# Transposes ahead of both down products, and a rearranged last expert and final norm

## The chip, the cores and the metric

The kernel runs on one core of one Trainium2 chip. The metric is the device time of one execution in microseconds. The core has a matrix engine (TensorE, "PE" in the profile), a vector engine (VectorE, "DVE"), a scalar engine (ScalarE, "ACT"), GpSimd ("POOL"), and SyncE ("SP"), whose queue issues nearly all DMAs here. Matrix products take a stationary operand of up to 128 rows (the contracted dimension) by 128 columns and a moving operand of up to 512 columns, and write into one of 8 banks of the accumulator memory (PSUM), which is `ps[:, bank, :]` in the code. A tile of 64 columns or 64 rows uses half of the array.

## The reference, cut to what matters

One encoder layer on 256 tokens of width 1024, in float32: norm, one wide projection, attention and a recurrent branch, merge, output projection, residual. Then the part that fills most of the time, a mixture of 32 experts, 4 of them for each token, and a last norm:

```python
h = rmsnorm(x, norm2_g);  logits = h @ w_router + b_router
top_val, top_idx = top_k(logits, 4);  gates = softmax(top_val)
for each expert e, on the tokens routed to it:
    gu  = xb @ w_gu[e] + b_gu[e]              # 1024 -> 2048
    g, u = split(gu);  g = minimum(g, 7);  u = clip(u, -7, 7)
    act = g * sigmoid(1.702 * g) * (u + 1)
    y  += gate * (act @ w_down[e] + b_down[e])   # 1024 -> 1024, added at the token's row
x = x + y
return rmsnorm(x, final_g)
```

Every expert's weights are 12 MiB (8 for `w_gu`, 4 for `w_down`), so 384 MiB of weights are read from the chip's memory once.

## The kernel before, in words

The mixer in front of the experts takes the first 240 us or so. All weights come in chunks of 2 MiB, 128 partitions by 16 KiB. Expert e has six: four of `w_gu`, two of `w_down`. They land in a ring of eight slots (`SLOT_ORDER`; the eighth is called `wide`), and SP issues the load of a chunk when the chunk that had its slot before has been used: it waits on `chunk_used[j]`, which TensorE raises after the products of a chunk (`expert_load` L293, `loop_load` L341). Two chunks of step 3 (`EXTRA`, numbers 18 and 19) have places of their own beside the ring. So in step 3 two gate/up products free no slot.

There is one step for each expert, `step(n, i)` on each engine; `i` counts modulo 4, and one set of 4 steps is a turn of a loop after the first 4. In step n TensorE does, in this order: gate/up product 0 of expert n (`gate_up`, L1333, 8 products of 128x64 tiles, two of them side by side), the gather of the tokens of expert n+1 by a 0/1 matrix (`gather_tile`, L1286), gate/up 1, in odd steps the transposes of the gate matrix (L1365) and two scatter products (L1305), gate/up 2, the transposes of the gathered tokens (`gathered_transposes`, L1300), in odd steps two more scatter products, gate/up 3, down product 0 of expert n-1 (`down`, L1342), the transposes of expert n's gate/up result (L1387), and down product 1 of expert n-1. The down products of an expert so run one step later than its gate/up. In step 0 (`first`), which has no down product, two products put the residual into banks 2 and 3 (`residual_in_bank`, L1264).

The transposes of L1387 wait until VectorE (L987) and ScalarE (L558) have each copied half of the gate/up result out of PSUM. VectorE then adds the bias and clamps (L993 to L998), ScalarE takes the sigmoid (L560), VectorE multiplies (L1001, L1005), and `act_ok` lets the next step's down products go. The next step's first gate/up product waits until L993 has read the transposes (`tp_read`).

Two experts share a `pair_out` tile, one in rows 0 to 63, one in rows 64 to 127, so that one scatter product of 128 rows adds two experts into banks 0 to 3, which hold the residual stream. For the last pair this happens at the end: TensorE does the down products of expert 31 (the second chunk in four quarters, L352), ScalarE and VectorE copy its result (L551, L1017), four scatter products follow (L1305), and then the final norm: ScalarE squares a tile of 128x1024 with a sum (L577), VectorE adds epsilon and inverts (L594, L595), ScalarE takes the root (L371), VectorE multiplies by root and gain (L1024), and SP stores 256 KB at a time (L357).

Order on each engine is that of its program. SP's queue is in order too.

Of the kernel before, what the change touches and what calls it, by code (L numbers as in the profile page):

```python
# [19 lines left out]
P = 128  # L20
# [35 lines left out]
def encoder_layer(nc, x, consts, squares, rows, pre, w_lru, w_gu, w_down, b_down, out):  # L56
# [5 lines left out]
    with ctx:  # L62
# [104 lines left out]
        bdn, gateT = pair_out[1][0:NE, :], sgT[1][0:NE, :, :]  # L167

# [42 lines left out]
        fin_ok, zeros = sem("fin_ok"), sem("zeros_ok")  # L211
        mix_part = sem("mix_part")
        last_in = [sem(f"last_quarter_in{r}") for r in range(4)]
        last_out = sem("last_out_v")
# [55 lines left out]
        LAST_SLOT = SLOT_ORDER[-3 % SLOTS]  # L270
        LAST_AFTER = (lambda nj: (nj[0] + (1 if nj[1] < 4 else AHEAD), nj[1]))(divmod(1 - SLOTS, PER))
# [7 lines left out]
        def _(sp):  # L279
# [69 lines left out]
            loop_load(n_pass, 0, 0, 4, NE - 1)  # L349
            sp.wait_ge(chunk_used[LAST_AFTER[1]], sp.snap(n_pass + LAST_AFTER[0]))  # L350
            for r in range(4):
                sp.dma_start(slot(LAST_SLOT)[:, r * D:(r + 1) * D],  # L352
                             expert_src(NE - 1, 5)[:, r * D:(r + 1) * D]).then_inc(last_in[r], 16)
# [8 lines left out]
        def _(act):  # L362
# [183 lines left out]
            def down_copy(n, i, bank=6, sides=range(2)):  # L546

                at_least(dn_done, n + 1 + AHEAD)
                rs = slice(64 * (i % 2), 64 * (i % 2) + 64)
                for side in sides:  # L550
                    nc.scalar.activation(pair_out[i // 2 % 2][rs, side * BANK:(side + 1) * BANK],  # L551
                                         ps[64 * side:64 * side + 64, bank, :], ACT.Copy).then_inc(out_ok, 1)
# [20 lines left out]
            down_copy(n_pass - 1, UNROLL - 1, 4, [0])  # L573

            for t in range(T):
                act.wait_ge(y_ok, 2 * t + 2)
                nc.scalar.activation(lruA[:, t * D:(t + 1) * D].rearrange("p (b n) -> p b n", b=2),  # L577
                                     ps[:, 2 * t:2 * t + 2, :], ACT.Square,
                                     accum_out=ssum[:, t:t + 1]).then_inc(sq_sum, 1)
                root(4 + t, slice(t, t + 1))  # L580

        @block.vector
        def _(dve):
# [389 lines left out]
            def step(n, i):  # L973
# [11 lines left out]
                scale_gathered(n + 1, i + 1)  # L985
                dve.wait_ge(gu_done, n1)
                nc.vector.tensor_copy(gu_sb[:, 0:BANK], ps[:, 4, :]).then_inc(gu_v, 1)  # L987
                dve.wait_ge(tp_ps, n1)
# [26 lines left out]

            dve.wait_ge(dn_done, dve.snap(n_pass + AHEAD))
            nc.vector.tensor_copy(pair_out[1][64:128, BANK:2 * BANK], ps[64:128, 4, :]).then_inc(last_out, 1)  # L1017
            dve.wait_ge(late_in, 32)
            for t in range(T):
                inverse_variance(ssum[:, t:t + 1], 2 * T + t + 1)  # L1020
                dve.wait_ge(rstd_ok, 4 + t)
                for h in range(2):
                    cols = slice(h * BANK, (h + 1) * BANK)
                    nc.vector.scalar_tensor_tensor(out=x_sb[:, t, cols], in0=ps[:, 2 * t + h, :], scalar=rstd[:, t:t + 1],  # L1024
                                                   in1=fin_g[:, cols], op0=ALU.mult, op1=ALU.mult).then_inc(fin_ok, 1)
# [3 lines left out]
        def _(pe):  # L1029
# [323 lines left out]
            def step(n, i, first=False):  # L1353
# [16 lines left out]
                if first:  # L1370
                    residual_in_bank(2)
                    residual_in_bank(3)
                gathered_transposes(n + 1)
# [4 lines left out]
                if not first:  # L1378
                    at_least(act_ok, n)
                    if i % 2 == 1:  # L1380
                        at_least(sg_ok, n + 3)
                    at_least(out_ok, n * 2 + 1)
                    down(n, i, 0, 4)
# [5 lines left out]
                if not first:  # L1389
                    down(n, i, 1, 5)  # L1390
# [22 lines left out]
            down(n_pass, 0, 0, 0, 4)  # L1413
# [74 lines left out]
```

## Time and profile before

| | |
|---|---|
| time, median of 3 runs | 1166.57 us |
| the three runs | 1162.07, 1166.57, 1167.43 us |
| span of the profiled execution (first to last instruction) | 1161.2 us |
| TensorE busy | 93% |
| VectorE, ScalarE busy | 33%, 20% |
| read from the chip's memory | 438.46 MB, 378 GB/s over the span |
| mean granted TensorE clock | 0.994 |

The profiled execution gives its span, 1161.2 us, and no time of its own beside it; of the timed runs the lowest, 1162.07 us, is 0.9 us above this span, and the other two are 5.4 and 6.2 us above it. A row of a timeline has start, duration, engine, line, operation, output and inputs, number of instructions, and in brackets the idle time before and what ended it. A float32 product is two instructions. Durations of a group overlap the next one's start by about 0.15 us (the end of the last product is counted with its way through the array), so that the time a group takes in a busy stretch is read from start to start.

### The profile page before, as it was taken

What the parts mean: (1) busy time and instruction counts of PE and PEld (TensorE: products, weight loads), DVE (VectorE), ACT (ScalarE), POOL (GpSimd) and SP (SyncE); (2) the same over time, 40 slices, a digit from 0 to 9 for tenths busy, and PEclk for the clock granted to TensorE, in tenths of its full rate; (3) what the DMA queues carried; (4) which work ended last, traced back from release to release, by engine and by line L of the source; (5) the groups of instructions that cost most, each with busy time, mean ns of one, the idle gap of its engine ahead of it and who ended that gap; (6) DMA issues with size and microseconds to landing.
All of it is one profiled execution on the core that took longest, in us unless ns stands there. A gap on an engine that the chain in (4) does not pass through costs nothing.

```text
span 1161.2 us, 13145 instructions
## 1 busy us (share of the span) xinstructions
PE 1081.6 (93%) x5391; PEld 502.8 (43%) x5391; DVE 382.9 (33%) x671; ACT 234.2 (20%) x371; POOL 0.2 (0%) x4
## 2 busy tenths in 40 slices
PE   5998999989999999999998989898989898989997
PEld 5998789823333333333333323332333233323332
DVE  6996798532322222222121212121211212121122
ACT  5388843100111111111111111111110101010112
POOL 0000000000000000000000000000000000000000
PEclk9999999989999999999999999999999999999999
DMA  8543146998999999999999999999999999999996
GB/s 351 186 171 145 73 160 278 418 400 333 429 397 425 431 425 429 428 428 429 428 429 428 430 428 427 430 428 428 430 428 428 429 428 430 428 427 429 429 428 248
DMA packets 32618, 439.89 MB, mean 379 GB/s; under 512 B 3760, under 2 KB 3888, under 8 KB 5712
## 3 DMA queue, kind: packets, MB, share of 16 engines
q1 hardware_dynamic: 32112, 438.53, 89.9%
q10 hardware_dynamic: 480, 0.99, 0.2%
q8 instruction: 19, 0.31, 0.1%
q14 instruction: 7, 0.06, 0.0%
HBM read 438.46 MB, written 1.05 MB: 378 GB/s over the span
## 4 chain that ended last, share of the span: by engine, by line
PE 61%; DMA 33%; DVE 4%; ACT 1%; issue 1%; SPq 0%; DVEq 0%
DMA slot<-in_w_gu_dram 27%; PE ps L1333 25%; PE ps L1037 12%; PE ps L1342 10%; DMA slot<-in_w_down_dram 6%; PE ps L1305 4%; PE ps L1286 3%; PE ps L1300 1%; PE ps L1387 1%; DVE slot_r L627 1%; PE ps L1092 1%; PE ps L1135 1%; PE ps L1264 1%; PE ps L1156 1%; PE ps L1365 0%
## 5 line engine op out<-in xcount | busy, mean ns | idle before, releaser
L1333 PE MATMUL ps<-slot,lru 128*64 128x512 f32 x880 | 198.9, 595 | 21.0 <-DMA slot<-in_w_gu_dram 20.7
L1342 PE MATMUL ps<-slot,lru 128*64 128x512 f32 x896 | 203.3, 596 | 14.8 <-DMA slot<-in_w_down_dram 14.3
L1333 PE MATMUL ps<-slot,qT 128*64 128x512 f32 x880 | 202.1, 601 | 14.4 <-DMA slot<-in_w_gu_dram 12.9
L1333 PEld LDWEIGHTS ps<-slot,lru 128*64 128x64 f32 x880 | 62.7, 137 | 147.6 <-issue 113.5
L1333 PEld LDWEIGHTS ps<-slot,qT 128*64 128x64 f32 x880 | 62.5, 137 | 147.1 <-issue 134.9
L1342 PEld LDWEIGHTS ps<-slot,lru 128*64 128x64 f32 x896 | 62.3, 137 | 135.4 <-issue 117.1
L558 ACT ACTIVATE lru<-ps 128x512 f32<-128x512 f32 x32 | 19.1, 598 | 419.7 <-PE ps L1333 419.7
L993 DVE TENSOR_TENSOR lru<-ps,cst 128x1024 f32<-128x1024 f32 x32 | 39.2, 1225 | 141.5 <-PE ps L1387 141.5
L970 DVE TENSOR_SCALAR lru<-sq,x_sb,small 128x64 f32<-128x64 f32 x66 | 17.7, 312 | 188.1 <-PE ps L1286 188.1
L1037 PE MATMUL ps<-wide_r,slot_r 128*128 128x256 f32 x492 | 66.2, 286 | 0.2 <-DVE slot_r L627 0.2
L1305 PE MATMUL ps<-lru 128*128 128x512 f32 x136 | 63.9, 593 | 0.9 <-DVE lru L1017 0.9
L1286 PE MATMUL ps<-hn,lru 128*64 128x512 f32 x264 | 63.7, 600 | 0.9 <-DVE lru L907 0.9
L987 DVE COPY lru<-ps 128x512 f32<-128x512 f32 x32 | 22.1, 692 | 127.6 <-PE ps L1333 127.6
L1037 PEld LDWEIGHTS ps<-wide_r,slot_r 128*128 128x128 f32 x492 | 61.3, 191 | 4.6 <-issue 4.1
L560 ACT ACTIVATE lru<-lru 128x512 f32<-128x512 f32 x32 | 20.2, 632 | 198.3 <-DVE lru L997 198.3
L627 DVE TENSOR_TENSOR slot_r<-slot,slot_r 128x4096 fp32r<-128x4096 f32 (+1 forms) x14 | 59.7, 4268 | 0.3 <-ACT slot_r L386 0.2
L544 ACT ACTIVATE qT<-ps 128x512 f32<-128x512 f32 x33 | 19.7, 598 | 160.7 <-PE ps L1286 160.7
L937 DVE TENSOR_TENSOR qT<-ps,cst 128x512 f32<-128x512 f32 x16 | 11.1, 692 | 116.6 <-PE ps L1300 116.6
L386 ACT ACTIVATE slot_r<-slot 128x2048 fp32r<-128x2048 f32 (+1 forms) x24 | 43.1, 1838 | 22.1 <-DMA slot<-in_pre_dram 22.1
L551 ACT ACTIVATE lru<-ps 64x512 f32<-64x512 f32 x63 | 37.3, 592 | 39.4 <-PE ps L1342 38.7
L1387 PEld LDWEIGHTS ps<-sq,lru 128*128 128x128 f32 x256 | 30.9, 193 | 26.8 <-issue 25.2
L937 DVE TENSOR_TENSOR lru<-ps,cst 128x512 f32<-128x512 f32 x17 | 11.8, 692 | 89.5 <-PE ps L1300 89.5
(212 smaller groups left out, 905.1 us busy)
## 6 DMA issues: line engine op xcount, KB each, us to landing
slot<-in_w_gu_dram SPq DMA_DIRECT2D x110, 2048.0 KB, 34.9
slot<-in_w_down_dram SPq DMA_DIRECT2D x55, 2048.0 KB, 33.2
wide<-in_w_gu_dram SPq DMA_DIRECT2D x15, 2048.0 KB, 34.8
slot<-in_pre_dram SPq DMA_DIRECT2D x14, 2048.0 KB, 8.3
wide<-in_w_down_dram SPq DMA_DIRECT2D x8, 2048.0 KB, 35.3
slot<-in_w_lru_dram SPq DMA_DIRECT2D x2, 1024.0 KB, 13.3
wide<-in_w_gu_dram SPq DMA_DIRECT2D x2, 1024.0 KB, 14.8
late<-in_w_gu_dram SPq DMA_DIRECT2D x1, 2048.0 KB, 16.8
```

The costliest lines, as they stand in the source:

```text
L386: nc.scalar.activation(high(c)[:, i * w:(i + 1) * w], whole(c)[:, i * w:(i + 1) * w], ACT.Copy).then_inc(split_hi, 1)
L551: nc.scalar.activation(pair_out[i // 2 % 2][rs, side * BANK:(side + 1) * BANK], ps[64 * side:64 * side + 64, bank, :], ACT.Copy).then_inc( ...
L627: return nc.vector.tensor_tensor(dst, whole, hi.bitcast(f32), ALU.subtract)
L937: nc.vector.tensor_tensor(xgT[i % 2].rearrange("p (h k) n -> p k h n", h=2), ps[:, 7, :].rearrange("p (k h n) -> p k h n", k=KD // 2, h=2) ...
L987: nc.vector.tensor_copy(gu_sb[:, 0:BANK], ps[:, 4, :]).then_inc(gu_v, 1)
L993: nc.vector.tensor_tensor(gub.rearrange("p (j n) -> p j n", j=16), ps[:, 4:6, :].rearrange("p b (j n) -> p (b j) n", n=CAP), bias.unsqueez ...
L1037: ins = nc.tensor.matmul(dst, st[a], mv[b], start=start and q == 0 and k == 0, stop=stop and q == 2 and k == len(sides) - 1)
L1286: ins = nc.tensor.matmul(ps[64 * h:64 * h + 64, 7, :], sel_next[:, t, :], x2[:, t, h * BANK:(h + 1) * BANK], start=(t == 0), stop=(t == T ...
L1305: return nc.tensor.matmul(ps[:, n, :], sgT[pair][:, n // 2, :], pair_out[pair][:, (n % 2) * BANK:(n % 2 + 1) * BANK], start=False, stop=last)
L1333: ins = nc.tensor.matmul(ps[64 * side:64 * side + 64, 4 + b, :], xgT[i % 2][:, k, :], rows[r][:, o:o + BANK], start=(k == 0), stop=(k == K ...
L1342: ins = nc.tensor.matmul(ps[64 * side:64 * side + 64, bank, :], actT[(i - 1) % 2][:, k, :], w[:, r, side * BANK:(side + 1) * BANK], start= ...
L1387: ins = nc.tensor.transpose(ps[:, 4 + j // 4, j % 4 * P:(j % 4 + 1) * P], gu_sb[:, j::KD], ident)
```

## The change

In each expert step on TensorE the transposes of the gathered tokens move behind gate/up 3, the transposes of the gate/up result come directly after them, and both down products come behind these. On VectorE the copy of the gate/up half goes ahead of the scaling of the gathered tokens. In step 0 one residual product stands between the two sets of transposes and one behind them. At the end both chunks of the last `w_down` are loaded and multiplied in quarters; expert 30 is scattered alone, by four products of 64 rows, between quarters 2 and 3 of the last chunk; the gate matrix of expert 31 is made once more so that it stands in both halves of the rows; expert 31 is scattered as pairs of 64-row tiles, one in the upper rows for the left 512 columns and one in the lower rows for the right 512. The last norm squares 512 columns at a time and VectorE multiplies by the gain first (in place of one product by both factors) and by the root in a second turn.

```diff
         def landed(c):
             return slot_full[PLACE[c]], 16 * PLACE[:c + 1].count(PLACE[c])
-        LAST_SLOT = SLOT_ORDER[-3 % SLOTS]
-        LAST_AFTER = (lambda nj: (nj[0] + (1 if nj[1] < 4 else AHEAD), nj[1]))(divmod(1 - SLOTS, PER))
+        LAST_SLOTS = [SLOT_ORDER[(j - 2 - len(EXTRA)) % SLOTS] for j in range(2)]
+        LAST_AFTER = [(nj[0] + (1 if nj[1] < 4 else AHEAD), nj[1]) for nj in (divmod(j - SLOTS, PER) for j in range(2))]
         def expert_src(e, j):
             c = gu_chunk[e, j] if j < 4 else dn_chunk[e, j - 4]
...
                     e_before = sp.snap(sp.to_reg((n + i - 1) & (NE - 1)), min_val=0, max_val=NE - 1)
                     for j in range(PER):
                         loop_load(n, i, j, j, e if j < 4 else e_before)
-            loop_load(n_pass, 0, 0, 4, NE - 1)
-            sp.wait_ge(chunk_used[LAST_AFTER[1]], sp.snap(n_pass + LAST_AFTER[0]))
-            for r in range(4):
-                sp.dma_start(slot(LAST_SLOT)[:, r * D:(r + 1) * D],
-                             expert_src(NE - 1, 5)[:, r * D:(r + 1) * D]).then_inc(last_in[r], 16)
+            for j, (after, used) in enumerate(LAST_AFTER):
+                sp.wait_ge(chunk_used[used], sp.snap(n_pass + after))
+                for r in range(4):
+                    sp.dma_start(slot(LAST_SLOTS[j])[:, r * D:(r + 1) * D],
+                                 expert_src(NE - 1, 4 + j)[:, r * D:(r + 1) * D]).then_inc(last_in[4 * j + r], 16)
             for n in range(2 * T):
                 t, cols = n // 2, slice((n % 2) * BANK, (n % 2 + 1) * BANK)
                 sp.wait_ge(fin_ok, n + 1)
...
                 at_least(xg_ps, n + 1)
                 nc.scalar.activation(xg_sb, ps[:, 7, :], ACT.Copy).then_inc(xg_cp, 1)
-            def down_copy(n, i, bank=6, sides=range(2)):
+            def down_copy(n, i):
                 at_least(dn_done, n + 1 + AHEAD)
                 rs = slice(64 * (i % 2), 64 * (i % 2) + 64)
-                for side in sides:
+                for side in range(2):
                     nc.scalar.activation(pair_out[i // 2 % 2][rs, side * BANK:(side + 1) * BANK],
-                                         ps[64 * side:64 * side + 64, bank, :], ACT.Copy).then_inc(out_ok, 1)
+                                         ps[64 * side:64 * side + 64, 6, :], ACT.Copy).then_inc(out_ok, 1)
             def step(n, i, first=False):
...
                 for i in range(UNROLL):
                     step(n + i, i)
             load_sqrt_table(3)
-            down_copy(n_pass - 1, UNROLL - 1, 4, [0])
+            act.wait_ge(dn_done, act.snap(n_pass + AHEAD))
+            nc.scalar.activation(last_pair[0:64, :], ps[0:64, 4, :], ACT.Copy).then_inc(out_ok, 1)
             for t in range(T):
                 act.wait_ge(y_ok, 2 * t + 2)
-                nc.scalar.activation(lruA[:, t * D:(t + 1) * D].rearrange("p (b n) -> p b n", b=2),
-                                     ps[:, 2 * t:2 * t + 2, :], ACT.Square,
-                                     accum_out=ssum[:, t:t + 1]).then_inc(sq_sum, 1)
-                root(4 + t, slice(t, t + 1))
+                for h in range(2):
+                    if h == 1:
+                        act.wait_ge(fin_y, 2 * t + 1)
+                    nc.scalar.activation(lruA[:, t * D + h * BANK:t * D + (h + 1) * BANK], ps[:, 2 * t + h, :], ACT.Square,
+                                         accum_out=part_sum[:, 2 * t + h:2 * t + h + 1]).then_inc(sq_sum, 1)
+            for t in range(T):
+                act.wait_ge(var_inv, 4 + t)
+                nc.scalar.activation(rstd[:, t:t + 1], ssum[:, t:t + 1], ACT.Sqrt, scale=float(D)).then_inc(rstd_ok, 1)
         @block.vector
         def _(dve):
...
                     dve.wait_ge(sg_ps, n1)
                     nc.vector.tensor_copy(sgT[i // 2], ps[:, 6, 0:T * P].rearrange("p (t n) -> p t n", t=T)
                                           ).then_inc(sg_ok, 2)
-                scale_gathered(n + 1, i + 1)
                 dve.wait_ge(gu_done, n1)
                 nc.vector.tensor_copy(gu_sb[:, 0:BANK], ps[:, 4, :]).then_inc(gu_v, 1)
+                scale_gathered(n + 1, i + 1)
                 dve.wait_ge(tp_ps, n1)
                 if isinstance(n, int):
                     bias = cst[:, C_BGU + 16 * n:C_BGU + 16 * (n + 1)]
...
                     step(n + i, i)
+            for t in range(T):
+                nc.vector.tensor_scalar(sel_gate[:, t, 0:CAP], slotno[:, 0:CAP], rank_col[:, t, column(n_pass - 1)],
+                                        gate_col[:, t, column(n_pass - 1)], ALU.is_equal, ALU.mult).then_inc(sgate_ok, 1)
+            dve.wait_ge(sg_ps, dve.snap(n_pass + 1))
+            nc.vector.tensor_copy(last_sgT, ps[:, 7, 0:T * P].rearrange("p (t n) -> p t n", t=T)).then_inc(last_sg, 1)
             dve.wait_ge(dn_done, dve.snap(n_pass + AHEAD))
-            nc.vector.tensor_copy(pair_out[1][64:128, BANK:2 * BANK], ps[64:128, 4, :]).then_inc(last_out, 1)
+            nc.vector.tensor_copy(last_pair[64:128, :], ps[64:128, 4, :]).then_inc(last_out, 1)
             dve.wait_ge(late_in, 32)
-            for t in range(T):
-                inverse_variance(ssum[:, t:t + 1], 2 * T + t + 1)
+
+            def with_gain(t):
+                for h in (1, 0):
+                    cols = slice(h * BANK, (h + 1) * BANK)
+                    if h == 1:
+                        dve.wait_ge(y_ok, 2 * t + 2)
+                    else:
+                        dve.wait_ge(sq_sum, 2 * T + 2 * t + 1)
+                    nc.vector.tensor_tensor(x_sb[:, t, cols], ps[:, 2 * t + h, :], fin_g[:, cols],
+                                            ALU.mult).then_inc(fin_y, 1)
+
+            def last_variance(t):
+                dve.wait_ge(sq_sum, 2 * T + 2 * t + 2)
+                link(nc.vector.tensor_scalar(ssum[:, t:t + 1], part_sum[:, 2 * t:2 * t + 1], part_sum[:, 2 * t + 1:2 * t + 2],
+                                             D * EPS, ALU.add, ALU.add))
+                nc.vector.reciprocal(ssum[:, t:t + 1], ssum[:, t:t + 1]).then_inc(var_inv, 1)
+
+            def normalize(t):
                 dve.wait_ge(rstd_ok, 4 + t)
+                dve.wait_ge(fin_y, 2 * t + 2)
                 for h in range(2):
                     cols = slice(h * BANK, (h + 1) * BANK)
-                    nc.vector.scalar_tensor_tensor(out=x_sb[:, t, cols], in0=ps[:, 2 * t + h, :], scalar=rstd[:, t:t + 1],
-                                                   in1=fin_g[:, cols], op0=ALU.mult, op1=ALU.mult).then_inc(fin_ok, 1)
+                    nc.vector.tensor_scalar(x_sb[:, t, cols], x_sb[:, t, cols], rstd[:, t:t + 1], None,
+                                            ALU.mult).then_inc(fin_ok, 1)
+
+            with_gain(0)
+            last_variance(0)
+            with_gain(1)
+            last_variance(1)
+            normalize(0)
+            normalize(1)
         @block.tensor
...
                     scatter(1 - i // 2, 0)
                     scatter(1 - i // 2, 1)
                 gate_up(n, i, 2)
-                if first:
-                    residual_in_bank(2)
-                    residual_in_bank(3)
-                gathered_transposes(n + 1)
                 if i % 2 == 1:
                     scatter(1 - i // 2, 2)
                     scatter(1 - i // 2, 3)
                 gate_up(n, i, 3)
-                if not first:
-                    at_least(act_ok, n)
-                    if i % 2 == 1:
-                        at_least(sg_ok, n + 3)
-                    at_least(out_ok, n * 2 + 1)
-                    down(n, i, 0, 4)
+                gathered_transposes(n + 1)
+                if first:
+                    residual_in_bank(2)
                 at_least(gu_v, n + 1)
                 at_least(gu_a, n + 1)
                 for j in range(KD):
                     ins = nc.tensor.transpose(ps[:, 4 + j // 4, j % 4 * P:(j % 4 + 1) * P], gu_sb[:, j::KD], ident)
                 ins.then_inc(tp_ps, 1)
-                if not first:
-                    down(n, i, 1, 5)
+                if first:
+                    residual_in_bank(3)
+                    return
+                at_least(act_ok, n)
+                if i % 2 == 1:
+                    at_least(sg_ok, n + 3)
+                at_least(out_ok, n * 2 + 1)
+                down(n, i, 0, 4)
+                down(n, i, 1, 5)
             pe.wait_ge(sel_ok, 1)
             gather_tile(0)
...
                 for i in range(UNROLL):
                     step(n + i, i)
             pe.wait_ge(act_ok, pe.snap(n_pass))
-            down(n_pass, 0, 0, 0, 4)
-            for r in range(4):
-                pe.wait_ge(last_in[r], 16)
-                ins = down_rows(0, LAST_SLOT, 1, r, 4)
+            for j in range(2):
+                for r in range(4):
+                    pe.wait_ge(last_in[4 * j + r], 16)
+                    ins = down_rows(0, LAST_SLOTS[j], j, r, 4)
+                    if (j, r) == (0, 2):
+                        pe.wait_ge(sgate_ok, pe.snap(n_pass * T + T))
+                        pe.wait_ge(xg_ok, pe.snap(n_pass + 1))
+                        for t in range(T):
+                            dup = nc.tensor.transpose(ps[:, 7, t * P:(t + 1) * P], sel_gate[:, t, :], ident)
+                        dup.then_inc(sg_ps, 1)
+                    if (j, r) == (1, 1):
+                        pe.wait_ge(out_ok, pe.snap(n_pass * 2 + 1))
+                        for n in range(2 * T):
+                            nc.tensor.matmul(ps[:, n, :], sgT[1][0:CAP, n // 2, :],
+                                             pair_out[1][0:CAP, n % 2 * BANK:(n % 2 + 1) * BANK], start=False, stop=False)
             ins.then_inc(dn_done, 1)
             pe.wait_ge(out_ok, pe.snap(n_pass * 2 + 2))
             pe.wait_ge(last_out, 1)
-            for n in range(2 * T):
-                scatter(1, n, True).then_inc(y_ok, 1)
+            pe.wait_ge(last_sg, 1)
+            for t in range(T):
+                for h in range(2):
+                    rs = slice(64 * h, 64 * h + 64)
+                    nc.tensor.matmul(ps[:, 2 * t + h, :], last_sgT[rs, t, :], last_pair[rs, :],
+                                     start=False, stop=True).then_inc(y_ok, 1)
 # ---- launch: layouts only ----
```

## Rows read from the trace of the kernel before

**Rows 1.** The page, span in 40 equal slices: memory rate.
```profile
GB/s 351 186 171 145 73 160 278 418 400 333 429 397 425 431 425 429 428 428 429 428 429 428 430 428 427 430 428 428 430 428 428 429 428 430 428 427 429 429 428 248
```

**Rows 2.** Windows: stretch, length, busy time per engine, granted clock, DMA share, GB/s.
```profile
398.00:551.00 153.00, 153.00 (x706) 54.32 (x704) 33.50 (x66) 17.44 (x29) 0.00 (x0) 1.00 1.01 428
610.00:668.00 58.00, 52.76 (x239) 18.82 (x237) 11.90 (x23) 6.02 (x10) 0.00 (x0) 1.00 1.01 429
340.00:342.00 2.00, 2.00 (x12) 0.62 (x9) 0.00 (x0) 0.00 (x0) 0.00 (x0) 1.00 0.56 238
264.00:266.00 2.00, 2.00 (x7) 0.62 (x5) 1.63 (x3) 0.58 (x1) 0.00 (x0) 0.51 0.93 393
1147.00:1148.00 1.00, 1.00 (x8) 0.38 (x6) 0.00 (x0) 0.00 (x0) 0.00 (x0) 1.00 0.28 115
1157.00:1158.00 1.00, 0.00 (x0) 0.00 (x0) 0.73 (x3) 0.20 (x1) 0.00 (x0) 1.00 1.00 377
```

**Rows 3.** Waits of PE, 560 to 1095 us: total, times, longest.
```profile
PE ps L1333 <- DMA slot<-in_w_gu_dram: 32.2, 33, 1.3
```

**Rows 4.** Timeline of SP, 330 to 345 us: the one issue there.
```profile
341.79 0.33 SPq L293 DMA_DIRECT2D slot<-in_w_gu_dram  x1
```

**Rows 5.** Timeline of PE, steps 4 and 5, start of step 6.
```profile
346.26 3.60 PE L1333 MATMUL ps<-slot,lru 128*64 128x512 f32 x16
...
358.38 0.66 PE L1300 MATMUL ps<-sq,qT 128*128 128x128 f32 x4
358.96 3.65 PE L1333 MATMUL ps<-slot,lru 128*64 128x512 f32 x16
...
370.56 3.60 PE L1333 MATMUL ps<-slot,qT 128*64 128x512 f32 x16
...
398.81 0.60 PE L1333 MATMUL ps<-slot,lru 128*64 128x512 f32 x2
```

**Rows 6.** Timeline of PE, end of step 0 and start of step 1.
```profile
252.51 3.71 PE L1264 MATMUL ps<-hn,sq 128*128 128x512 f32 x4
...
256.59 3.65 PE L1333 MATMUL ps<-wide,lru 128*64 128x512 f32 x16
261.04 1.15 PE L1387 MATMUL ps<-sq,lru 128*128 128x128 f32 x8 [0.80 <-DVE lru L987]
263.70 5.35 PE L1333 MATMUL ps<-slot,qT 128*64 128x512 f32 x16 [1.52 <-DVE lru L993]
268.86 0.63 PE L1286 MATMUL ps<-hn,lru 128*64 128x512 f32 x2
```

**Rows 7.** Timeline of PE, step 31 to the last scatter.
```profile
1119.09 0.14 PEld L1333 LDWEIGHTS ps<-slot,qT 128*64 128x64 f32 x2 [0.32 <-DMA slot<-in_w_gu_dram]
...
1130.99 3.65 PE L1333 MATMUL ps<-slot,qT 128*64 128x512 f32 x16
...
1138.01 1.16 PE L1387 MATMUL ps<-sq,lru 128*128 128x128 f32 x8
1139.10 3.65 PE L1342 MATMUL ps<-wide,lru 128*64 128x512 f32 x16
...
1143.56 7.09 PE L1342 MATMUL ps<-slot,lru 128*64 128x512 f32 x32 [0.81 <-DMA slot<-in_w_down_dram]
...
1151.54 3.67 PE L1305 MATMUL ps<-lru 128*128 128x512 f32 x8 [0.89 <-DVE lru L1017]
```

**Rows 8.** Timeline of ACT, DVE and SP, the last norm.
```profile
1156.15 2.93 SPq L357 DMA_DIRECT2D out_dram<-x_sb  x4
1156.17 0.19 ACT L577 ACTIVATION_READ_ACCUMULATOR lru<-ps 128x1 f32 x1
...
1157.31 1.41 DVE L1024 SCALAR_TENSOR_TENSOR x_sb<-ps,small,lru 128x512 f32<-128x512 f32 x2 [0.27 <-ACT small L371]
```

**Rows 9.** The page, costliest groups: a copy and a scaling of 128x512.
```profile
L558 ACT ACTIVATE lru<-ps 128x512 f32<-128x512 f32 x32 | 19.1, 598 | 419.7 <-PE ps L1333 419.7
...
L997 DVE TENSOR_SCALAR lru<-lru 128x512 f32<-128x512 f32 x32 | 13.7, 427 | 1.1
```

More of the change, by code:

```diff
@@ L167, in encoder_layer @@
         bdn, gateT = pair_out[1][0:NE, :], sgT[1][0:NE, :, :]
+        part_sum = neg_max
+        last_pair, last_sgT = pair_out[0][:, 0:BANK], sgT[0]
         gv = gub.rearrange("p (j h n) -> p j h n", j=KD, h=2)
@@ L210, in encoder_layer @@
             sem(n) for n in ("g_clamped", "sigmoid_ok", "u_clamped", "gated_ok", "act_ok", "out_ok", "y_ok"))
-        fin_ok, zeros = sem("fin_ok"), sem("zeros_ok")
+        fin_y, fin_ok, zeros = sem("fin_y"), sem("fin_ok"), sem("zeros_ok")
         mix_part = sem("mix_part")
-        last_in = [sem(f"last_quarter_in{r}") for r in range(4)]
-        last_out = sem("last_out_v")
+        last_in = [sem(f"last_quarter_in{r}") for r in range(8)]
+        last_out, last_sg = sem("last_out_v"), sem("last_sgT_ok")
         block = ctx.enter_context(nc.Block())
```

## The prediction

> **What bounds the kernel now.** I read the memory rate over the span first [rows 1]. From the thirteenth slice to the last but one it stands at 425 to 431 GB/s; before that, between 232 and 348 us, it drops twice (333 and 397). Then two windows [rows 2]. From 398 to 551 us TensorE is busy all of the time and the DMA share is 1.01. From 610 to 668 us the DMA share is the same and TensorE has 5.2 of 58 us idle. So the weight stream runs without a gap in both, and TensorE, which is behind it at first, has caught up by 560 us and waits for chunks from then on [rows 3]. A pair of steps costs TensorE 52.55 us (346.26 to 398.81), of which the even one takes 24.30 and the odd one 28.25 [rows 5], a mean of 26.3. The stream needs 12 chunks of 2.097 MB at 428.5 GB/s, 58.7 us for a pair or 29.36 for a step. Between step 4 and the end, TensorE could be later by a good 1.8 us in each step without being the bound (from 346.26 to 1142.6 there are 28 steps, 28.4 us each, against 26.3, and the change adds 0.3, below).
>
> Three things therefore set the end: when the stream last ran dry, since from there it only flows; how long TensorE still works behind the last chunks; and the norm. The last dry place is at 340 to 343 us, where the DMA share of a window is 0.56 [rows 2] and SP issues a load at 341.79 after a long wait [rows 4]. It is the slot that down product 0 of step 3 sets free (two chunks of that step lie outside the ring and free nothing). At the other end TensorE waits for a gate/up chunk at 1119.09 and then works without a pause until a wait of 0.81 us ahead of 1143.56 [rows 7], while the stream is almost over by 1147 to 1148 [rows 2]. TensorE goes on to 1150.65. The last 7 us of products are TensorE's own.
>
> **Start, step 0.** Now gate/up 3 starts at 252.51, where the two residual products stand, instead of 256.59: 4.08 earlier [rows 6]. A gate/up group takes 3.5 from start to start (3.65 less the 0.15 of overlap), the transposes of the gathered tokens 0.58 (358.38 to 358.96 [rows 5]), a residual product 1.77 (half of the time from 252.51 to 256.59, less 0.58). Before, the transposes of the gate/up result followed 4.45 after the start of gate/up 3, with 0.80 idle for the copies; now gate/up, transposes and residual fill 5.85, so the wait is covered, and they start at 258.36. From these transposes to step 1's first product it was 2.66 (261.04 to 263.70), with 1.52 idle for VectorE's read; a residual product behind transposes of 1.09 (1138.01 to 1139.10 [rows 7]) fills 2.86. Step 1 begins at 261.2, 2.5 earlier.
>
> The group there took 5.35 in place of 3.65, and its window shows a granted clock of 0.51 (1.2 GHz) [rows 2, 6]. The engine had been idle for 0.80 and 1.52 just before, with only the transposes between. These idle times go, so I take the full clock: the next group starts 3.5 instead of 5.16 later, and the gain is 4.1. If the low clock stays it is 2.5.
>
> **Every further step.** The transposes of the result start 4.45 after gate/up 3 starts [rows 6], as the copies need that; 3.5 plus 0.58 of the moved transposes fill 4.08. So 0.37 is idle that the down product covered before. Two sets of the same tile shape now stand together, which spares a change of shape; I take 0.3 a step, with 0 and 0.5 as ends. VectorE's scaling of the gathered tokens comes later but is covered by both down products (7.0). The down products find their input from the step before, and the two copies of the down result are still made after the second. No DMA is added. What depends on the new place is the release of the slots: gate/up 3 frees its slot 0.58 earlier, down product 0 by 1.09 plus the wait later, down product 1 about 0.3 later.
>
> At the dry place: 4.1 gained, 3 steps of 0.3 lost (1, 2 and 3), 1.1 lost as the transposes stand ahead of down product 0. The issue at 341.79 comes 2.1 earlier, and the stream with everything that waits for it to 1119.09 moves by that. Ends: 0.5 (low clock) and 3.0 (no wait in the steps). The mean step of 26.3 becomes 26.6, still under 28.4, and costs nothing there.
>
> A page of the Trainium skill, "TensorE: Matmul & The Clock Gate" (Part 4, PE-mode transpose), says that transposes do not count as activity for the clock in the way that matmuls do. By that rule the change brings two sets together with a wait between them in every step, and the clock could fall there; the rival on the clock is priced below.
>
> **Tail, from step 31.** Rows 7 give it. Before: gate/up 3 at 1130.99, transposes at 1138.01, second down product at 1139.10, its successor possible at 1142.6, started at 1143.56 when the chunk had landed, 7.09, end 1150.65. After, on the same clock: gate/up 3 at 1130.41 (0.58 of transposes gone ahead of it), transposes 4.45 later at 1134.86, down products from 1135.95 to 1142.95. The quarters of the first last chunk are in by 1143.5 and three come before, so nothing waits for the 0.81 any more. Then TensorE has eight quarters, 6.95; two transposes of the gate matrix, a quarter of eight, 0.3, and 0.1 for the shape; and the four scatter products of expert 30. These have 64 rows, but 512 moving columns as before and all in the same half of rows, so I give them the time of the 128-row ones, 3.55 of 3.67 [rows 7]. Sum 142.95 + 6.95 + 0.4 + 3.55 + 0.15 of drain = 1154.0, or 3.35 later than 1150.65. Ends: 1.6, if 64 rows cost half, and 3.9, if each of the four changes of shape costs another 0.14. The eight quarters have 4 KB rows; SP may stand at the issue, but nothing is behind it there save the stores.
>
> The step was made to take those products out of the very end. There, four products side by side in two halves of rows cost half of 3.67, a gain of 1.8 for the last data. The same 3.55 now stands before, and no supply wait covers it.
>
> **Norm.** From the scatter's start S (1151.54, 0.89 after the down product) to VectorE's end it took 7.18 [rows 7, 8]. After: the first tile is complete at S+1.0, the second at 1.9. ScalarE's half square is 0.60 [rows 9] and 0.19 to read the sum [rows 8], 0.8 with the handover; VectorE's product from PSUM 0.70 (half of 1.41). The two alternate over the two halves: VectorE to 1.7, ScalarE to 2.65, VectorE's sums to 3.05, gain product to 3.75, the fourth square to 4.65, sums to 5.1; the second turns, 0.43 each with overlap [rows 9], end at 6.7. That is 0.45 less. But the first store goes at 5.6, where it went at 4.6 (1156.15), and four stores of 0.7 (262 KB at 377 GB/s [rows 2]) then stand in a row of 2.8: 0.45 more by the stores. I take nothing, with 0.5 either way. That 64-row tiles in different halves run together no row shows; in turn they take 3.67 and the second tile is 0.9 later than ScalarE comes to it. Column tiles do run in pairs: 16 instructions of L1333 take 3.65, where 8 of L1305 take 3.67.
>
> **Sum.** -2.1 (start) + 3.35 (tail) + 0 (norm) = +1.3 us, on the profiled span of 1161.2: 1162.5. The span is 5.4 below the median of the runs, and I move the median by the same: 1166.57 + 1.3 = 1168.
>
> **The rivals.**
> (a) The low clock at the start of step 1 stays, or comes elsewhere among the first steps: start 0.5 instead of 2.1. +2.9, 1169.5. For it: no row tells how little idle time suffices. Against: in the stream-paced steps idle times of 1.3 [rows 3] stand once in some groups and the mean clock is still 1.00 [rows 2]. 15%.
> (b) The row tiles don't run in pairs: +0.9 on the norm, +2.2, 1169. 8%.
> (c) The tail costs nothing: the scatter of expert 30 falls into time in which TensorE waits for quarters. Then -2.1, 1164.5. Against it, no wait in the 23 us after 1119.09 but one of 0.81. 10%.
> (d) Faster by over 0.5%: the stream loses 10.5 us against 428.5 GB/s in the four slices from 232 to 348 (28.5, 95.5 and 31.5 GB/s missing of slices of 29.03 us, [rows 1]). If an earlier gate/up 3 closed most of it and not one gap alone, 6 to 9 us, less the tail: 1160. Against: the last gap hangs on down product 0 of step 3, whatever comes before. 7%.
> (e) Slower: the clock falls within the steps. Place: the two sets of transposes with the wait, in steps 4 to 31; price 1.7 (5.35 less 3.65 [rows 6]) for each group that runs at 1.2 GHz. One a step gives 28.3, still under 28.4, and costs only 1.7 or so at the tail. It decides above 1.8 us a step; two groups make 30.0, 28 steps of 1.6, +45 us, 1212. For it, the row at 263.70. Against, the stretch without ordinary products is 0.58 + 0.37 + 1.09 = 2.0, and at 263.70 it was 3.5 (0.80 + 1.15 + 1.52). 5%.
> The rest, 55%, is the forecast.
>
> **How the numbers follow.** The forecast with its ends (start -3.0 to -0.5, tail 1.6 to 3.9, norm -0.5 to 0.5) runs from -1.9 to +3.9 and with (b) to +4.8; the three runs of before spread over 5.4 us, and a median of three may fall on either side of it. I give 1162 to 1173. Under 0.5% (5.8 us) the measurement of this kernel can't tell a change from none. Faster by more: (d) and a little of (c), 8%. Slower by more: (e), and a tenth of the rest by a bad sum of its upper ends, 11%. Same: 81%.
>
> **What would show it.** In the changed kernel's profile: step 1's first group at about 261.2 of 3.65 at clock 1.00, and none at 0.51 near 264; an idle time of 0.3 to 0.4 ahead of the transposes of each step, ended by VectorE's copy; the issue after the two extra chunks at 339.7, and the waits for chunks at the same phase as before but 2 us earlier; no wait for a quarter, the end of the down products 10.6 to 11.5 after the second down product of step 31 ends; a scatter of 8 instructions at the end in 1.9. I am wrong if the start gains under 0.5 or over 3, if TensorE waits for quarters, or if steps in the stream-paced stretch take other than 58.7 a pair.

## The result, and the profile after

The changed kernel takes 1167.13 us (median of 20 runs, 1163.53 to 1170.3), the kernel before 1164.44 us in the 20 runs beside it (1161.6 to 1167.43). The ratio is 1.003, with a 95% interval of 1.0021 to 1.0039: some 3.5 us (2.4 to 4.5) slower, and under the 0.5% that I had called no change. I had forecast +1.3 us and 1168. That 1168 lies close to 1167.13 is luck: the median of three runs that I started from (1166.57) is 2.1 us above the median of 20 (1164.44), and the change is 2.2 us larger than I had. One execution of 2252.93 us (the kernel before) and one of 2841.81 us (steps 1 to 31 alone) are far outside the others and are left out of every median, mean and ratio here. The two profiled executions are only 0.5 apart, 1161.2 and 1161.7, so at least one of them must differ from the usual run, and the question is where.

To compare them I cut the span at events that both have: SP's issue of the first `w_down` chunk (it waits for step 0's first product), SP's issue after the two extra chunks, the first gate/up product of step 31, the end of the last down product (the copy on VectorE starts 0.05 later), and the end of the span. SP's timeline of the kernel before, with the first of these; the second is [rows 4]:

```profile
244.04 5.48 SPq L293 DMA_DIRECT2D slot<-in_w_down_dram  x2
```

SP's timeline of the changed kernel:

```profile
243.22 5.48 SPq L295 DMA_DIRECT2D slot<-in_w_down_dram  x2
...
338.75 0.33 SPq L295 DMA_DIRECT2D slot<-in_w_gu_dram  x1
```

From one to the other it is 97.75 before and 95.53 after: 2.2 less. TensorE at the end of step 0, changed kernel, for [rows 6]:

```profile
251.60 3.60 PE L1369 MATMUL ps<-wide,lru 128*64 128x512 f32 x16
255.13 0.66 PE L1336 MATMUL ps<-sq,qT 128*128 128x128 f32 x4
255.62 1.89 PE L1300 MATMUL ps<-hn,sq 128*128 128x512 f32 x2
257.34 1.07 PE L1416 MATMUL ps<-sq,lru 128*128 128x128 f32 x8
258.24 1.89 PE L1300 MATMUL ps<-hn,sq 128*128 128x512 f32 x2
260.06 3.65 PE L1369 MATMUL ps<-slot,qT 128*64 128x512 f32 x16
263.54 1.89 PE L1322 MATMUL ps<-hn,lru 128*64 128x512 f32 x8
```

No row has a bracket, so both idle times of [rows 6] are covered. Step 1's first group takes 3.65 in place of 5.35. Then the tail. The first product of step 31 and VectorE's copy behind the last down product, in the kernel before, which [rows 7] does not show:

```profile
1114.28 3.65 PE L1333 MATMUL ps<-slot,qT 128*64 128x512 f32 x16 [1.33 <-DMA slot<-in_w_gu_dram]
...
1150.70 0.69 DVE L1017 COPY lru<-ps 64x512 f32<-64x512 f32 x1 [7.64 <-PE ps L1342]
```

The changed kernel, step 31 and the end:

```profile
1111.01 3.65 PE L1369 MATMUL ps<-slot,qT 128*64 128x512 f32 x16 [1.34 <-DMA slot<-in_w_gu_dram]
...
1130.91 0.66 PE L1336 MATMUL ps<-sq,qT 128*128 128x128 f32 x4
...
1131.78 1.17 PE L1416 MATMUL ps<-sq,lru 128*128 128x128 f32 x8 [0.21 <-DVE lru L993]
1132.87 3.65 PE L1378 MATMUL ps<-slot,lru 128*64 128x512 f32 x16
...
1136.36 3.60 PE L1378 MATMUL ps<-wide,lru 128*64 128x512 f32 x16
...
1139.79 2.75 PE L1378 MATMUL ps<-slot,lru 128*64 128x512 f32 x12
...
1142.46 0.44 PE L1457 MATMUL ps<-sq,lru 128*128 128x128 f32 x2
1142.83 2.80 PE L1378 MATMUL ps<-slot,lru 128*64 128x512 f32 x12
1145.56 3.70 PE L1462 MATMUL ps<-lru 64*128 64x512 f32 x8
1149.18 1.94 PE L1378 MATMUL ps<-slot,lru 128*64 128x512 f32 x8
...
1151.97 1.99 PE L1471 MATMUL ps<-lru 64*128 64x512 f32 x8 [0.84 <-ACT lru L576]
```

Expert 30's scatter stands at 1145.56 and takes 3.62 to the next start, although its stationary tile has 64 rows; expert 31's, in pairs, takes 1.99 for as many instructions. None of the rows with quarters (1139.79, 1142.83, 1149.18) has a bracket: TensorE waits for no quarter. From 1111.01 to the end of the down products (1151.12) it is 40.11; before, from 1114.28 to 1150.65, it was 36.37. That is 3.74 more.

The stream in those last microseconds (window of the changed kernel: stretch, length, busy times, clock, DMA share, GB/s) had ended by 1145:

```profile
1145.00:1150.00 5.00, 5.00 (x16) 1.76 (x14) 0.00 (x0) 0.00 (x0) 0.00 (x0) 1.00 0.00 0
```

The norm, for [rows 8]:

```profile
1151.17 0.69 DVE L1029 COPY lru<-ps 64x512 f32<-64x512 f32 x1 [7.81 <-PE ps L1378]
...
1156.74 1.67 DVE L1053 TENSOR_SCALAR x_sb<-x_sb,small 128x512 f32<-128x512 f32 x4
...
1157.25 1.81 SPq L359 DMA_DIRECT2D out_dram<-x_sb  x4
```

VectorE ends 6.44 after the start of the last scatter, where it was 7.18; the first store goes 5.28 after that start, where it was 4.61. From the copy to the end of the span it is 10.53, and 10.50 before.

All kernels of this study, by these cuts (us, from the timelines of one profile each; up to the first issue the code is the same in all of them):

| kernel | to first issue | to issue after extras | to step 31 | to end of down | copy to end |
|---|---|---|---|---|---|
| before | 244.04 | 97.75 | 772.49 | 36.37 | 10.50 |
| before, second profile | 249.03 | 96.06 | 772.51 | 36.37 | 10.48 |
| changed | 243.22 | 95.53 | 772.26 | 40.11 | 10.53 |
| order alone | 244.07 | 95.53 | 772.27 | 36.37 | 10.51 |
| step 0 alone | 245.15 | 93.21 | 772.82 | 36.37 | 10.50 |
| steps 1 to 31 alone | 245.89 | 98.36 | 772.14 | 36.36 | 10.50 |
| new end alone | 249.13 | 96.07 | 772.63 | 40.22 | 10.60 |
| norm alone | 245.56 | 96.05 | 772.28 | 36.37 | 11.49 |
| changed, old norm | 245.45 | 95.50 | 772.45 | 40.09 | 9.66 |
| changed, no early scatter | 244.29 | 95.48 | 772.14 | 36.32 | 10.62 |
| order and quarters | 247.52 | 95.52 | 772.33 | 35.81 | 10.47 |
| step 0 and quarters | 244.03 | 93.21 | 772.74 | 35.91 | 10.46 |
| quarters alone | 245.88 | 96.05 | 772.58 | 35.91 | 10.53 |

The time from the issue after the extras to step 31 is 772.1 to 772.8 in all profiles, whatever the order of the steps: the weight stream flows from its last dry place, and little else counts in between (the six profiles with the new order in steps 1 to 31 average 772.3, the other seven 772.6). The first column, 243.2 to 249.1 for one and the same code, is what the profiles differ by beyond the edits.

The other columns can be held against the measured times. For each kernel I take the sum of its differences from the second profile of before, without the first column. It lies inside the interval of the ratio for ten of the eleven kernels that have one (for the changed kernel, about +3.0 against 2.4 to 4.5). The exception is the new order alone, below.

### The profile page after: what moved, and what is told of

It is laid out like the page before. It is cut to its first block, busy times and chain, and to the rows that moved or that the text cites. A ratio compares the mean times of both kernels' runs of the same rounds, so it can differ in the third digit from the quotient of the medians.

```text
span 1161.7 us, 13186 instructions
## 1 busy us (share of the span) xinstructions
PE 1084.5 (93%) x5401; PEld 502.0 (43%) x5401; DVE 382.3 (33%) x678; ACT 234.3 (20%) x375; POOL 0.2 (0%) x4
## 4 chain that ended last, share of the span: by engine, by line
PE 64%; DMA 29%; DVE 5%; ACT 1%; issue 1%; SPq 0%; DVEq 0%
DMA slot<-in_w_gu_dram 28%; PE ps L1369 27%; PE ps L1073 12%; PE ps L1378 10%; PE ps L1341 5%; PE ps L1322 3%; PE ps L1416 2%; DVE lru L993 1%; DVE slot_r L634 1%; PE ps L1128 1%; PE ps L1171 1%; PE ps L1300 1%; PE ps L1192 1%; PE ps L1401 1%; DMA x_sb<-in_x_dram 0%
## 5 line engine op out<-in xcount | busy, mean ns | idle before, releaser
L1416 PE MATMUL ps<-sq,lru 128*128 128x128 f32 x256 | 36.8, 287 | 6.4 <-DVE lru L993 6.4
L1369 PE MATMUL ps<-wide,lru 128*64 128x512 f32 x144 | 32.7, 596 | 6.2 <-DMA wide<-in_w_gu_dram 6.2
L1073 PE MATMUL ps<-slot_r 128*128 128x256 f32 (+1 forms) x256 | 37.6, 290 | 0.0
```

The source lines that it names most:

```text
L1073: ins = nc.tensor.matmul(dst, st[a], mv[b], start=start and q == 0 and k == 0, stop=stop and q == 2 and k == len(sides) - 1)
L1369: ins = nc.tensor.matmul(ps[64 * side:64 * side + 64, 4 + b, :], xgT[i % 2][:, k, :], rows[r][:, o:o + BANK], start=(k == 0), stop=(k == K ...
L1416: ins = nc.tensor.transpose(ps[:, 4 + j // 4, j % 4 * P:(j % 4 + 1) * P], gu_sb[:, j::KD], ident)
```

## The experiments

Each was run 7 to 12 times beside 22 to 35 runs of the kernel before on the same chip, except the single look.

**The new order alone** (steps as changed, end as before).

```diff
  step(), TensorE: gate_up 2, [scatter 2, 3], gate_up 3,
- gathered_transposes ahead of gate_up 3, transposes between down 0 and down 1
+ gathered_transposes, transposes of gate/up, down 0, down 1
```

> The kernel before with the new order of the steps alone (step 0's too); last expert, chunks and norm as before. Theory A (the start gains, the tail loses): faster than before by 2 to 3 us, ratio 0.998; the load after the two extra chunks is issued 2 to 3 us earlier than 341.79, and the last down product ends by as much before 1150.65, less 0.3. Rival B (the new order costs in the steps, by the clock or by waits, and the tail costs little): slower than before by 1 to 3 us, and granted clocks under 1.00 within steps 4 to 31.

Measured: 0.998 (0.9968 to 0.9992), 1160.96 us. The issue after the extras comes at 339.60, step 31 and the end follow by the table, and the clock is full in steps 4 to 31 (mean 0.997 over the span). Theory A holds in sign and rival B falls: the kernel is not slower. The size is open. The ratio says 2.3 us (0.9 to 3.7), and the cuts give 0.7 against the second profile of before and 2.4 against the first, the one with the slow group. Five of its seven runs have a mean clock of 0.996 or 0.997, against 3 of the 30 runs of before at 0.996 or more, so part of the gain goes with the clock; where in the span the clock fell in those runs, no trace shows.

**Step 0 alone.**

```diff
+ if first:
+     gate_up 2, gate_up 3, gathered_transposes, residual_in_bank(2),
+     transposes of gate/up, residual_in_bank(3); return
  (steps 1 to 31 in the order of before)
```

> The kernel before with the new order in step 0 alone (the residual products cover the two waits there); steps 1 to 31 and the end as before. Theory A: the whole gain of 4 us at the start stays, since nothing is given back in steps 1 to 3 and down product 0 of step 3 frees its slot no later: issue at 337 to 338 in place of 341.79, ratio 0.9965. If the stream's last dry place did not decide (rival), the ratio is 1.000, the same as if nothing was done.

Measured: 0.9976 (0.9964 to 0.9988), 1161.17 us, a gain of 2.8 and not 4. The stretch is 93.21. Against the first profile of before that is 4.54 less, as expected; against the other profiles with the old step 0 and the old order (96.05 to 96.07) it is 2.85. The time (a gain of 1.4 to 4.2) agrees with the second. The issue after the extras comes at 338.36 and not at 337 to 338, as this profile's first issue was 1.1 later.

**The new end alone.**

```diff
+ all hunks of the change but those in step() of TensorE and VectorE
```

> The kernel before with all of the new end (both last chunks in quarters, expert 30's scatter by itself before the last two quarters, 64-row pairs for expert 31, norm in two turns), steps in the old order. Theory A: slower by 3.0 to 3.8 us, ratio 1.003; scatter of expert 30 3.6 in front, 1.8 less behind, last data 1.7 to 2 later for TensorE plus the transposes, and 0.8 waited less. Rival B (the tail costs little): ratio 1.000 to 1.001.

Measured: 1.0033 (1.0021 to 1.0046), 1167.88 us. From step 31's start to the end of the down products it is 3.85 more, at the upper end of A's 3.0 to 3.8. This kernel also has the old step 0, with the same two idle times, and its step 1 (timeline of TensorE):

```profile
266.14 1.16 PE L1423 MATMUL ps<-sq,lru 128*128 128x128 f32 x8 [0.80 <-DVE lru L994]
268.82 3.65 PE L1369 MATMUL ps<-slot,qT 128*64 128x512 f32 x16 [1.52 <-DVE lru L1000]
```

The same 0.80 and 1.52 as [rows 6], and 3.65 in place of 5.35.

**The norm alone.**

```diff
- Square of ps[:, 2t:2t+2, :]; root; scalar_tensor_tensor by rstd and fin_g
+ Square of ps[:, 2t+h, :] for h in 0, 1; with_gain, last_variance, normalize
  (scatter: four products of 128 rows)
```

> The kernel before with the norm in two turns alone (squares of 512 columns, gain first, root second), behind the old scatter of four 128-row products. Theory A: within 0.5 us of before, ratio 1.000; from scatter start to VectorE's end 6.7 to 7.2. Rival: the norm is where the loss is, 1.5 us or more, since the first store goes 1 us later and four stores stand in a row.

Measured: 1.0013 (1.0004 to 1.0022), 1165.73 us. VectorE and SP at the end:

```profile
1150.31 0.69 DVE L1022 COPY lru<-ps 64x512 f32<-64x512 f32 x1 [7.64 <-PE ps L1370]
...
1156.75 1.68 DVE L1045 TENSOR_SCALAR x_sb<-x_sb,small 128x512 f32<-128x512 f32 x4
...
1157.26 1.82 SPq L358 DMA_DIRECT2D out_dram<-x_sb  x4
```

VectorE is done 7.28 after the scatter's start (1151.15), 0.1 later than before, and the stores, whose first goes 1.5 later, end 1.0 later. The interval and the profile agree on a loss; my 0.5 was too little, and the rival's loss by the stores is there, at 1.0 and not 1.5.

**The changed kernel with the old norm.**

```diff
- with_gain, last_variance, normalize; two squares of 512 a tile
+ one square of 1024 a tile; root; scalar_tensor_tensor by rstd and fin_g
```

> The changed kernel with the norm of before (squares of 1024 columns, one product by root and gain), behind the 64-row pairs. Theory A, mended after the norm alone had cost 1.0 to 1.5: the norm in two turns loses about 1 us wherever it stands and the pairs gain about as much, so this is 1 us faster than the changed kernel: ratio to before 1.002, and from VectorE's last copy of the down result to the end of the span 9.5 in place of 10.53. Rival: the norm in two turns was the right partner of the pairs, whose tiles come close together, and this is no faster (10.5 or more).

Measured: 1.0015 (1.0001 to 1.0028), 1165.99 us; copy to end 9.66. So the pairs gain 0.84 with the old norm (10.50 to 9.66) and the norm in two turns loses 0.87 behind them (9.66 to 10.53) and 0.99 without them.

**The changed kernel without expert 30's scatter** (its part of the sum is left out).

```diff
-                    if (j, r) == (1, 1):
-                        pe.wait_ge(out_ok, ...)
-                        for n in range(2 * T):  nc.tensor.matmul(ps[:, n, :], sgT[1][0:CAP, ...], ...)
```

> The changed kernel without the four scatter products of expert 30 (its contribution is left out of the output). Theory A: they are bare time of TensorE behind the stream, so 3.5 us go: ratio to before 1.000 to 0.9995, and 3.6 less from the start of the last eight quarters to the end of the down products. Rival: TensorE would otherwise wait for the last quarters, and under 1.5 us go.

Measured: 0.9997 (0.9983 to 1.0011), 1163.23 us; step 31 to the end of the down products 36.32 in place of 40.11, 3.8 less. The output lacks expert 30's part, so this is a kernel for the time alone. The four products are bare time, all of it.

**The new order with quarters, old scatter and norm.**

```diff
- loop_load(n_pass, 0, 0, 4, NE - 1)      # SP: first chunk whole
- down(n_pass, 0, 0, 0, 4)                # TensorE
+ for j in range(2): for r in range(4): quarter load; wait last_in[4*j+r]; down_rows(0, LAST_SLOTS[j], j, r, 4)
```

> The kernel before with the new order of the steps and both last chunks in quarters; scatter of 128 rows and norm as before. Theory A: the order's gain (0.998 by itself) and up to 0.4 more, since TensorE waited 0.34 for the first of the two chunks with the new order: ratio 0.9975 to 0.998. Rival: eight loads of 4 KB rows slow the stream or hold SP, and 1 us or more of the gain is lost.

Measured: 0.9979 (0.9964 to 0.9995), 1161.09 us; 35.81 to the end of the down products. The eight small loads cost nothing to be seen.

**Step 0 and quarters** (the two edits above, on the kernel before).

> The kernel before with the new order in step 0 alone and both last chunks in quarters; scatter and norm as before. Theory A: the gain of step 0 (0.9976 by itself) plus the 0.8 that TensorE waits for the first of the two last chunks in the old order: ratio 0.997, the fastest of all. Rival: the transposes' result comes too late for the first quarter in the old order, and nothing is added.

Measured: 0.9972 (0.9957 to 0.9987), 1160.38 us. This is the lowest ratio of all, 0.28% under before (its interval overlaps that of step 0 alone) and, by the two ratios, 0.6% under the changed kernel. By the table the quarters gain 0.46 (36.37 to 35.91), not 0.8. TensorE, at 1138.80 in its profile, waits 0.36 for VectorE's last product of the activation in place of 0.81 for the chunk, as my own rival had it in part:

```profile
1138.80 7.09 PE L1345 MATMUL ps<-slot,lru 128*64 128x512 f32 x32 [0.36 <-DVE lru L1008]
```

**Steps 1 to 31 alone, old step 0.**

```diff
+ if first: order of before; else: order of the change
```

> The kernel before with the new order in steps 1 to 31 and the old step 0. Theory A: what the new order costs without what step 0 gives: from the first down load to the load after the extra chunks 96.05 + 2.3 = 98.4 us at full clock (97.75 + 2.3 = 100.1 if step 1's first group is slow), the rest as before: 2 us slower, ratio 1.002. Rival: the new order by itself is free in the time, and the ratio is 1.000.

Measured: 1.0027 (1.0014 to 1.004), 1166.51 us. The stretch is 98.36, as worked out (98.4), and step 1's first group takes 3.65.

**Quarters alone** (the quarters' edit on the kernel before).

> The kernel before with both last chunks in quarters and nothing else. Theory A: 0.4 us faster (TensorE starts on the first quarter when the activation is there instead of when the chunk is in): ratio 0.9996, not to be told from 1.000. Also a look at whether step 1's first group takes 5.35 or 3.65 with the old step 0: if the slow group of the first profile belongs to the order, it takes 5.35; if it is chance, 3.65 as in the two kernels so far.

Measured: 1.0001 (0.9988 to 1.0015), 1164.15 us; step 1's first group 3.65.

**The kernel before once more, one look.**

> The kernel before once more, for the record of step 1's first group alone: 5.35 as in the first profile if the slow clock comes from the order of step 0, 3.65 at clock 1.00 if it is chance from run to run.

Measured: 1166.44 us in its one run, and in the profile

```profile
266.03 1.15 PE L1387 MATMUL ps<-sq,lru 128*128 128x128 f32 x8 [0.80 <-DVE lru L987]
268.69 3.65 PE L1333 MATMUL ps<-slot,qT 128*64 128x512 f32 x16 [1.52 <-DVE lru L993]
```

with the granted clock at full over the idle times and the start of the group (and in every window of 1 us from 246 us on):

```profile
264.00:266.00 2.00, 1.23 (x6) 0.14 (x2) 0.69 (x1) 0.70 (x2) 0.00 (x0) 1.00 0.82 352
266.00:268.00 2.00, 1.15 (x8) 0.96 (x8) 0.79 (x1) 1.18 (x1) 0.00 (x0) 1.00 0.93 287
268.00:270.00 2.00, 1.30 (x6) 0.57 (x8) 1.86 (x4) 0.63 (x1) 0.00 (x0) 1.00 0.95 385
```

Six profiles are of kernels with the old step 0: the two of before, the new end, the norm, steps 1 to 31 and the quarters alone. Their idle times are the same to 0.01 us. One shows the slow group (5.35 at 1.2 GHz), the first, and five don't.

## Why the prediction was right, and where it was not

**Right: what bounds the kernel.** The stream's last dry place sets all that follows, and a change within the steps that keeps TensorE under the stream's pace costs nothing later: 772.1 to 772.8 in every profile.

**Right with a wrong size: the start.** I had step 1 begin 2.5 earlier, each new step cost 0.3 and the place of the transposes 1.1. Steps 1 to 31 alone lose 98.36 - 96.06 = 2.30 (I had 0.9 + 1.1 = 2.0), step 0 alone gains 96.06 - 93.21 = 2.85 (I had 2.5). What was wrong is the further 1.7 for the slow group. I took a slow clock in one profile as a cost that the old order has, since idle times stood before it. The idle times alone don't bring it: it was seen in one profile of six. Without it the start gains 96.06 - 95.53 = 0.53, not 2.1; with it, as in the two first profiles, 2.22. This is the term that failed. How often the timed runs of before have the slow group is not known. If they always had it, the change would come to +1.6 by the sum below, outside the measured 2.4 to 4.5; the interval allows it in less than half of them, if nothing else differs. My rival (a), at 15%, had the same 0.5 for the start, but by another way: a slow clock that stays in the changed kernel. Its profile has none there.

**Right: the tail.** 3.35 forecast, 3.74 measured in the changed kernel, 3.85 in the end alone. The 64-row products cost what 128-row ones do (3.62 of 3.67, I had 3.55), and taken out they give back 3.8. Of the 0.4 between, 0.3 is in the last eight quarters with what stands among them (11.33 from 1139.79 to 1151.12, I had 11.05) and 0.1 in step 31 itself (28.78 to the first quarter, I had 28.67). The eight quarters took 7.34 (2.67 + 2.73 + 1.94) where I had 7.10 with the drain. For the four changes of tile shape my upper end had 0.14 each, a price that no row shows; together they cost 0.3 at most. Rival (c), that waits would cover it, falls.

**Right by two wrong parts that cancel: the norm.** I had 0 for both together and it is +0.03. The parts are a gain of 0.84 by the pairs, which shows that tiles in different halves of the rows do run together, against rival (b), and a loss of 0.87 by the two turns. I had the stores' 0.45 but set a gain of VectorE's time against it that only the pairs bring (7.28 behind the old scatter, 6.44 behind the pairs). That the sum of the two came out right is luck.

**Sum.** With the start at full clock: -0.53 + 3.74 + 0.03 = +3.2 us; measured 3.5 (2.4 to 4.5). With my slow group it would be +1.6, and the two profiles by themselves have +0.5, as the changed kernel's one also reached step 0 0.8 sooner and its stream was 0.2 shorter (-0.82 - 2.22 - 0.23 + 3.74 + 0.03 = +0.50). The changed kernel's profile is of its fastest run of 20 (1163.53).

**Rival (e)**, a clock that falls within the steps with two sets of transposes side by side: no. In the changed kernel and in the order alone the granted clock is 1.00 in each window of 1 us from 261 to 1140 us. The rule of the Trainium skill ("TensorE: Matmul & The Clock Gate", Part 4, PE-mode transpose), that transposes do not count as activity in the way that matmuls do, is not refuted by that, nor borne out: the two sets (0.66 and 1.17, with 0.21 idle between) lowered the clock in no step, and the rule decided nothing here. The wait added to each step was 0.21 and not 0.37 (row at 1131.78), the price of a step the 0.3 that I had: a pair takes 53.14 in the changed kernel (gather to gather, two rows of TensorE's timeline) where it took 52.55.

```profile
292.27 1.89 PE L1322 MATMUL ps<-hn,lru 128*64 128x512 f32 x8
...
345.41 1.89 PE L1322 MATMUL ps<-hn,lru 128*64 128x512 f32 x8
```

Rival (d) fell: the largest gain of any kernel here is 3.3 us (step 0 and quarters), and the stretch from the issue behind the extras to step 31 stayed at 772.1 to 772.8 in all of them.

## What to carry to other kernels

Where a transfer stream is the bound, read the place where it last ran dry; an edit counts there and behind the last transfer, not in the steps between. Work taken out of the last chain must go where the engine waits; put ahead of the last products on an engine that is already late, it only changes its place, and here a product of 64 rows without a partner in the other half cost as much as one of 128 (3.62 against 3.67 for four). A slow group in one profile is no term of a sum before a second profile, or another kernel with the same code, has shown it again: look at more than one.

## What the runs showed of the hardware that I had not expected

The same idle times (0.80 and 1.52, with 1.15 of transposes between) ended once in a group at 1.2 GHz and five times at full clock. The same code before step 0 took 243.2 to 249.1 us to the first issue, and there too the clock differs. In windows of 1 us every profile has a stretch at 1.2 GHz somewhere from 233 to 246 us, near idle times of TensorE of 1.01 and 0.85 us. All 13 have an idle time of 3.14 to 3.16 that ends between 101 and 104 us; five have a stretch at 1.2 GHz there, eight don't. The first profile of before is the only one with such a stretch at step 1. The two with least time at 1.2 GHz ahead of the first issue (changed, and changed without the early scatter) reach it at 243.2 and 244.3, the three with most (before's second, the new end alone, order and quarters) at 247.5 to 249.1.

The mean granted clock goes with the time: of 87 runs of the kernel before, the 11 at 0.991 average 1166.8 us, the 39 at 0.994 1164.2, and the 8 at 0.998 1161.3. What decides whether the clock falls at such a place wasn't tried and stays open.
